# Attention: who normalises the probabilities, and which value products are rounded

## The chip, the cores and the metric

The kernel runs on one core of a Trainium2 chip. The time is what the device takes for one execution, in microseconds (us). Five engines work side by side, each with its own queue, in order: TensorE (PE) multiplies matrices and transposes, VectorE (DVE), ScalarE (ACT) and GpSimd (POOL) work element by element, and SyncE (SP) starts transfers. They wait for each other through semaphores. In this kernel GpSimd works on tiles in SBUF alone; VectorE and ScalarE also read the matmul results in PSUM.

## The reference, cut to what matters

The program is one decoder layer over 1024 tokens of width 1024: an RMS norm and an input projection, a retention part (8 heads), an attention part with three branches (8 query heads in 2 groups of key and value heads), an output projection, a gated MLP with a convolution, a gate from per-layer inputs, and a last norm. The change touches only the attention part:

```python
def masked_softmax(s, mask):
    s = jnp.where(mask, s.astype(jnp.float32), -jnp.inf)
    m = jnp.max(s, axis=-1, keepdims=True)
    m = jnp.where(jnp.isfinite(m), m, 0.0)
    e = jnp.exp(s - m)
    return e / jnp.maximum(jnp.sum(e, axis=-1, keepdims=True), 1e-30)
...
o = (gates[..., 0:1] * unblock(o_c) + gates[..., 1:2] * unblock(o_s)
     + gates[..., 2:3] * unblock(o_w))
```

Branch 0 attends to 63 compressed blocks, branch 1 to the selected blocks (with 16 blocks of 64 tokens and the 16 best chosen these are all tokens so far), branch 2 to a window of 512 tokens. Each has its own softmax, its own sum, and its own gate.

## The kernel before, in words

The work is in stages: projection with retention woven in, compression of keys and values, attention, output projection, MLP, final gate. The attention stage lies from about 447 to 771 us of the profiled execution.

It is tiled into 16 rounds `v`: token tile `t = v // 2` (128 queries) and key group `g = v % 2` (4 heads). Each round has 8 softmax steps `i`: head `r_ = i // 2`, and `i % 2` is 0 for branch 1 (up to 1024 columns) and 1 for branches 2 (up to 640 columns) and 0 (63 columns) together. All steps of all rounds have a running number `n = 8v + i`, and the whole stage is written as a list of slots, one for each `n`, by `plan_attention`. Every engine walks through the same slots in order.

For one step TensorE computes the scores into PSUM (`qk`, line 1206 and after), VectorE takes the row maxima and makes the bias from them (`row_max`, `exp_bias`), ScalarE writes `exp` into the SBUF tile `prob` and its row sum into `den` (`exponentials`; the accumulator read is a record of its own). One slot later VectorE guards the sum against zero (line 1673), takes the reciprocal (1678), and multiplies the probabilities in place by the reciprocal and the gate (1688, 1692 and 1695 for the three branches). `prob` has two places, for odd and for even rounds.

The value product comes one round later. Each tile of 128 keys (the last one of a round has the 63 compressed blocks) is a turn and an output. The turn (`p_turn`) is four transposes on TensorE, into one of three PSUM banks, recorded under line 1146. It waits on `norm_done` until all 8 steps of its round are normalised. Then the tile takes one of two ways:

- whole: ScalarE copies the bank to `ptw` in f32 (line 862), and TensorE multiplies in full f32, two records under line 1262
- not whole: ScalarE copies it rounded to `pth` (line 862), VectorE writes the remainder to `ptl` (`p_low`, recorded under line 1612), and TensorE makes two products of the rounded kind (lines 1264 and 1265)

Which way tile `j` of a round takes is said by one line:

```python
            return st[0] == "turn_p" and st[2] % 5 in (0, 2)
```

A round has 3, 5, 7, 9, 11, 12, 13, 14 tiles for token tiles 0 to 7. The turns and outputs of round `v` are spread over the slots `8v + 9` to `8v + 16`; in each slot TensorE first does these, then the scores of the step after. The scores of step `n` wait for the exponentials of step `n - 2`, whose PSUM banks they take.

GpSimd adds the squares at the start (line 609), issues the stores and loads of the projection and retention stages, and takes powers (-0.5) for the norms (lines 611, 643, 663, 667). In the attention stage it has nothing to do.

Of the kernel before, what the change touches and what calls it, by code (L numbers as in the profile page):

```python
# [7 lines left out]
ALU = mybir.AluOpType  # L8
ACT = mybir.ActivationFunctionType
AX_X = mybir.AxisListType.X  # L10
F32 = mybir.dt.float32
# [4 lines left out]
P = 128  # L16
S = 1024
D = 1024
NT = S // P
# [4 lines left out]
G = 2  # L24
RG = QH // G
CMP_BLOCK, CMP_STRIDE, CMP_HID = 32, 16, 256
NCMP = (S - CMP_BLOCK) // CMP_STRIDE + 1
CJ = CMP_BLOCK // 2
WIN_T = 4
# [5 lines left out]
SCALE = HD ** -0.5  # L35
# [13 lines left out]
C_DIAG = C_ID + P  # L49
# [5 lines left out]
C_CD = C_QD + RH  # L55
C_INV = C_CD + RH
C_HALF = C_INV + NA
C_N = C_HALF + NT


def constants():

    c = np.zeros((P, C_N), np.float32)
    p, f = np.arange(P)[:, None], np.arange(P)[None, :]
    c[:, C_ID:C_ID + P] = p == f
    c[:, C_DIAG:C_DIAG + P] = np.where(f <= p, 0.0, MASKED)
    c[:, C_FAR:C_FAR + P] = np.where(f > p, 0.0, MASKED)
    n = np.arange(NCMP)[None, None, :]
    t = np.arange(NT)[None, :, None] * P + np.arange(P)[:, None, None]
    cm = np.zeros((P, NT, HD))  # L70
    cm[:, :, :NCMP] = np.where(n * CMP_STRIDE + CMP_BLOCK - 1 <= t, 0.0, MASKED)
    c[:, C_CMP:C_CMP + NT * HD] = cm.reshape(P, -1)
    log_g = np.log1p(-np.exp2(-5.0 - np.arange(RH)))
    for h in range(RH):
        c[:, C_DT + h * P:C_DT + (h + 1) * P] = np.where(f >= p, np.exp(np.maximum(f - p, 0) * log_g[h]), 0.0)
        c[:, C_KD + h] = np.exp((P - 1.0 - np.arange(P)) * log_g[h])
        c[:, C_QD + h] = np.exp((np.arange(P) + 1.0) * log_g[h])
        c[:, C_CD + h] = np.exp(P * log_g[h])
    for at, half, theta in ((0, ROPE_R, 10000.0), (ROPE_R, ROPE_N, 500000.0)):
        e = -np.arange(half, dtype=np.float32) / np.float32(half)  # L80
        c[:, C_INV + at:C_INV + at + half] = np.power(np.float32(theta), e)
    c[:, C_HALF:] = -0.5
    return c


# [23 lines left out]
def build(nc, xt, x, pt, pos, cst_d, wmix_d, wffn_d, gnw, w_in, cpos, ck_w1, ck_w2, cv_w1, cv_w2,  # L109
# [8 lines left out]
    with ctx:  # L118
        def sem(name):
            return ctx.enter_context(nc.semaphore(name))  # L120
# [102 lines left out]
        comb = a.put("comb", [P, 2, 2 * P], F32)  # L223
        mx = a.put("mx", [P, 4, 2], F32)
        nb = a.put("nb", [P, 4, 2], F32)
        den = a.put("den", [P, 4, 2], F32)
        rd = a.put("rd", [P, 4, 2], F32)
        rd2 = a.put("rd2", [P, 4, 2], F32)
        assert a.at <= 229344, a.at


# [63 lines left out]
        cst_in = sem("cst_in")  # L295
        xt_in, w_in_s = sems("xt_in", XR), sems("w_in", RR)

        cst_r, cst_m = sem("cst_r"), sem("cst_m")
        xh_done, sq_done, xl_done = sem("xh_done"), sem("sq_done"), sem("xl_done")
        acc_done, ss_done, ms_done, rstd_done = sem("acc_done"), sem("ss_done"), sem("ms_done"), sem("rstd_done")  # L300
        red_done, sin_done = sem("red_done"), sem("sin_done")
# [50 lines left out]
        def ret_slots(s, k, table):  # L352
# [17 lines left out]
        tr_full, tr_h, tr_l = sem("tr_full"), sem("tr_h"), sem("tr_l")  # L370
        qk_done, nb_done, exp_done, norm_done, pv_done = (
            sem("qk_done"), sem("nb_done"), sem("exp_done"), sem("norm_done"), sem("pv_done"))
        swap_done, csum_done, nsah_done, nsal_done = sem("swap_done"), sem("csum_done"), sem("nsah_done"), sem("nsal_done")

        h_in, wfb_in = sem("h_in"), sem("wfb_in")
# [55 lines left out]
        def whole(st):  # L431

            return st[0] == "turn_p" and st[2] % 5 in (0, 2)

        outs_of = {(v, j): n for n, (v, j) in enumerate(st[1:] for st in plan if st[0] == "output")}

# [165 lines left out]
        def _(pool):  # L604
# [48 lines left out]
            for s in range(NS + 1):  # L653
                for k in range(NK):
# [3 lines left out]
                        ret_load(0)  # L658
                    ret_slots(s, k, table)

            for t in range(NT):
                pool.wait_ge(hms_done, t + 1)
                nc.gpsimd.tensor_tensor(hst[:, 2, t:t + 1], hst[:, 1, t:t + 1], cst[:, C_HALF:C_HALF + 1], ALU.pow) \
                    .then_inc(hrs_done, 1)
# [6 lines left out]
        def _(act):  # L671
# [164 lines left out]
            def exponentials(v, i):  # L836
                n, t = 2 * RG * v + i, v // G
                r_, br = divmod(i, 2)
                act.wait_ge(nb_done, n + 1)
                if v >= 2:  # L840
                    act.wait_ge(tr_full, turns_of["turn_p", v - 2, len(key_tiles(v - 2)) - 1] + 1)
                s_, pr = ps[:, 2 * br:2 * br + 2, :].rearrange("p a n -> p (a n)"), prob[:, v % 2, r_]
                m = n % 4
                if br == 0:
                    nc.scalar.activation(pr[:, 0:(t + 1) * P], s_[:, 0:(t + 1) * P], ACT.Exp, bias=nb[:, m, 0:1],
                                         scale=SCALE, accum_out=den[:, m, 0:1]).then_inc(exp_done, 1)
                else:
                    w = (t - max(0, t - WIN_T) + 1) * P
                    nc.scalar.activation(pr[:, S:S + w], s_[:, 0:w], ACT.Exp, bias=nb[:, m, 0:1], scale=SCALE,
                                         accum_out=den[:, m, 0:1])  # L850
                    at = S + (WIN_T + 1) * P
                    nc.scalar.activation(pr[:, at:at + NCMP], s_[:, 5 * P:5 * P + NCMP], ACT.Exp, bias=nb[:, m, 1:2],  # L852
                                         scale=SCALE, accum_out=den[:, m, 1:2]).then_inc(exp_done, 1)

            def p_high(st):
                at = place_of[st]
# [150 lines left out]
        def _(pe):  # L1007
# [32 lines left out]

            def sum_squares():
                pe.wait_ge(acc_done, NK - 1)
                pe.wait_ge(cst_m, 1)
                for t in range(NT):
                    mm = nc.tensor.matmul(ps[:, 4, t:t + 1], xacc[:, t * P:(t + 1) * P], ones[:], start=True, stop=True)
                mm.then_inc(ss_done, 1)
# [188 lines left out]
            def p_turn(st):  # L1235
                v, j = st[1:]
                _, _, at, w = key_tiles(v)[j]
                pe.wait_ge(norm_done, 2 * RG * (v + 1))
                turn_free(st)
                for r_ in range(RG):  # L1240
                    mm = transpose_f(ps[0:w, turn_bank(st), r_ * P:(r_ + 1) * P], prob[:, v % 2, r_, at:at + w])
                mm.then_inc(tr_full, 1)
# [158 lines left out]
        def _(dve):  # L1401
# [8 lines left out]
            def mark(ins):  # L1410

                count[0] += 1
                ins.then_inc(dve_chain, 1)
                return count[0]

            dve.wait_ge(cst_in, 48)
            chain(nc.vector.memset(ones[:], 1.0))
            nc.vector.tensor_copy(ident_b[:], ident_f).then_inc(cst_m, 1)
            nc.vector.tensor_copy(masks_b[:], cst[:, C_DIAG:C_DT]).then_inc(cst_m, 1)

            def split_w(j):
                dve.wait_ge(wh_done, j + 1)
# [244 lines left out]
                dve.wait_ge(dve_chain, maxima)  # L1667
                nc.vector.tensor_scalar(nb[:, m, 0:w], mx[:, m, 0:w], FLOOR, -SCALE, ALU.max, ALU.mult).then_inc(nb_done, 1)

            def guard_sum(v, i):  # L1670
                n, w = 2 * RG * v + i, 1 + i % 2
                dve.wait_ge(exp_done, n + 1)
                return mark(nc.vector.tensor_scalar(rd[:, n % 4, 0:w], den[:, n % 4, 0:w], 1e-30, None, ALU.max))

            def invert_sum(v, i, guarded):
                m, w = (2 * RG * v + i) % 4, 1 + i % 2
                dve.wait_ge(dve_chain, guarded)
                return mark(nc.vector.reciprocal(rd2[:, m, 0:w], rd[:, m, 0:w]))

            def normalize(v, i, inverted):  # L1680

                n, (t, g_), (r_, br) = 2 * RG * v + i, divmod(v, G), divmod(i, 2)
                m, hd = n % 4, g_ * RG + r_
                dve.wait_ge(dve_chain, inverted)
                pr = prob[:, v % 2, r_]
                if br == 0:
                    p_ = pr[:, 0:(t + 1) * P]
                    nc.vector.tensor_scalar(p_, p_, rd2[:, m, 0:1], gates[:, t, hd, 1:2], ALU.mult, ALU.mult).then_inc(norm_done, 1)
                else:
                    width = (t - max(0, t - WIN_T) + 1) * P  # L1690
                    p_ = pr[:, S:S + width]
                    nc.vector.tensor_scalar(p_, p_, rd2[:, m, 0:1], gates[:, t, hd, 2:3], ALU.mult, ALU.mult)
                    at = S + (WIN_T + 1) * P
                    p_ = pr[:, at:at + NCMP]
                    nc.vector.tensor_scalar(p_, p_, rd2[:, m, 1:2], gates[:, t, hd, 0:1], ALU.mult, ALU.mult).then_inc(norm_done, 1)

            def p_low(st):
                at = place_of[st]
                w = key_tiles(st[1])[st[2]][3]
# [28 lines left out]
            for n, slot in enumerate(slots):  # L1728
                lows = [st for st in slot if st[0] in ("turn_p", "turn_ret") and not whole(st)]
                if n < 2 * RG * NV:  # L1730
                    maxima = row_max(*divmod(n, 2 * RG))
                if 0 < n <= 2 * RG * NV:
                    guarded = guard_sum(*divmod(n - 1, 2 * RG))
                if n < 2 * RG * NV:
                    exp_bias(*divmod(n, 2 * RG), maxima)
                if 0 < n <= 2 * RG * NV:
                    inverted = invert_sum(*divmod(n - 1, 2 * RG), guarded)
                for st in lows:
                    {"turn_p": p_low, "turn_ret": ret_low}[st[0]](st)
                if 0 < n <= 2 * RG * NV:  # L1740
                    normalize(*divmod(n - 1, 2 * RG), inverted)
                for st in slot:
                    {"split_q": q_split_low, "sum": add_parts, "combine": nsa_low}.get(st[0], skip)(st)

# [175 lines left out]
```

## Time and profile before

| | |
|---|---|
| median of 3 runs | 1783.72 us (1783.25 to 1783.78) |
| span of the profiled execution | 1782.5 us, first to last instruction |
| its own time | not given beside the span; the runs' times are 0.75 to 1.28 us above it |
| TensorE busy | 1653.7 us (93%) |
| VectorE busy | 1054.2 us (59%) |
| ScalarE busy | 628.0 us (35%) |
| GpSimd busy | 109.5 us (6%) |
| attention stage | about 447 to 771 us |

How to read it: the busy time of TensorE comes from modelled ends of pipelined matmuls, and short overlaps are in it. The shares are means over stages with different limits, so the stage's own windows count more than they do. "E <- R" in a view is an engine that sat idle until R was done.

### The profile page before, as it was taken

How to read it: one execution, taken by the hardware profiler on the slowest of the kernel's cores; microseconds unless marked ns; L12 is line 12 of the kernel's file. 1: busy time of each engine (PE TensorE's matmuls, PEld its weight loads, DVE VectorE, ACT ScalarE, POOL GpSimd, SP SyncE). 2: the span in 40 equal slices, each digit the busy share in tenths (PEclk: the TensorE clock that was granted, in tenths of full speed). 3: DMA queues.
4: the chain of work that ended last, by engine and by line, in shares of the span. 5: the costliest groups of instructions: out<-in, count | busy, mean ns of one | idle time of the engine just before them, and what ended most of it. 6: DMA issues, size and time to landing. Idle time of an engine off the chain costs nothing.

```text
span 1782.5 us, 22209 instructions
## 1 busy us (share of the span) xinstructions
PE 1653.7 (93%) x8157; PEld 1334.8 (75%) x8157; DVE 1054.2 (59%) x2073; ACT 628.0 (35%) x1161; POOL 109.5 (6%) x132
## 2 busy tenths in 40 slices
PE   3999999998789999989899999999999999996894
PEld 1888888888656776668788888888888888885673
DVE  7542556565799999842545556556555555556233
ACT  5103443344577777731422212212212212213121
POOL 4101112121000000000100000000000000000002
PEclk9999999999699999999899999999999999998997
DMA  5233323225000000130211211211111112102002
GB/s 188 90 100 120 102 93 110 78 80 200 24 22 16 13 13 1 65 138 0 75 55 36 71 35 38 68 35 46 60 35 52 54 35 57 61 1 95 0 36 82
DMA packets 47850, 110.57 MB, mean 62 GB/s; under 512 B 8864, under 2 KB 17056, under 8 KB 47776
## 3 DMA queue, kind: packets, MB, share of 16 engines
q1 hardware_dynamic: 40352, 85.47, 14.8%
q0 software_dynamic: 7424, 24.12, 4.0%
q8 instruction: 45, 0.74, 0.2%
q14 instruction: 29, 0.24, 0.0%
HBM read 89.65 MB, written 19.92 MB: 61 GB/s over the span
## 4 chain that ended last, share of the span: by engine, by line
PE 81%; DVE 11%; ACT 3%; DMA 2%; issue 2%; POOL 0%; POOLq 0%; SPq 0%; DVEq 0%; ACTq 0%
PE ps L1325 27%; PE ps L1011 13%; PE ps L1012 13%; PE ps L1013 13%; PE ps L1146 3%; PE ps L1262 3%; PE ps L1219 2%; PE ps L1225 1%; PE ps L1264 1%; PE ps L1016 1%; DVE xtl L1444 1%; PE ps L1169 1%; DVE wl L1424 1%; DVE htl L1612 1%; PE ps L1265 1%
## 5 line engine op out<-in xcount | busy, mean ns | idle before, releaser
L1798 DVE TENSOR_TENSOR h<-h,ps 128x512 f32<-128x512 f32 x352 | 236.1, 685 | 156.1 <-PE ps L1013 154.8
L1325 PE MATMUL ps<-hth,wuh 128*128 128x512 f32 x704 | 218.6, 392 | 3.1 <-DVE wul L1612 3.1
L1325 PE MATMUL ps<-htl,wuh 128*128 128x512 f32 x704 | 219.0, 392 | 0.0
L1325 PE MATMUL ps<-hth,wul 128*128 128x512 f32 x704 | 218.6, 392 | 0.0
L1011 PE MATMUL ps<-wh,xth 128*128 128x512 f32 (+1 forms) x448 | 187.5, 419 | 31.1 <-DVE wl L1424 29.7
L1013 PE MATMUL ps<-wh,xtl 128*128 128x512 f32 (+1 forms) x448 | 171.2, 382 | 0.0
L1012 PE MATMUL ps<-wl,xth 128*128 128x512 f32 (+1 forms) x448 | 170.7, 381 | 0.0
L952 ACT ACTIVATE ffh<-ffa 128x1024 fp32r<-128x1024 f32 x22 | 23.3, 1059 | 385.1 <-DVE ffa L1815 385.1
L1325 PEld LDWEIGHTS ps<-hth,wuh 128*128 128x128 f32 x704 | 132.4, 188 | 32.9 <-issue 3.3
L1325 PEld LDWEIGHTS ps<-hth,wul 128*128 128x128 f32 x704 | 132.7, 188 | 29.4
L1325 PEld LDWEIGHTS ps<-htl,wuh 128*128 128x128 f32 x704 | 132.5, 188 | 28.8
L1011 PE MATMUL ps<-wdh,ffh 128*128 128x512 f32 x352 | 139.5, 396 | 4.3 <-DVE ffl L1612 4.3
L1012 PE MATMUL ps<-wdl,ffh 128*128 128x512 f32 x352 | 140.3, 399 | 0.0
L1013 PE MATMUL ps<-wdh,ffl 128*128 128x512 f32 x352 | 139.5, 396 | 0.0
L1011 PEld LDWEIGHTS ps<-wh,xth 128*128 128x128 f32 x448 | 85.8, 192 | 44.4 <-issue 26.8
L1805 DVE SCALAR_TENSOR_TENSOR act__149<-gate,taps,act__149 128x1024 f32<-128x1024 f32 x22 | 28.3, 1285 | 129.2 <-ACT act__149 L945 129.2
L1146 PE MATMUL ps<-cst,prob 128*128 128x128 f32 (+1 forms) x592 | 89.3, 279 | 9.7 <-DVE retl L1612 7.8
L1013 PEld LDWEIGHTS ps<-wh,xtl 128*128 128x128 f32 x448 | 85.5, 191 | 16.2
L1219 PE MATMUL ps<-aks,aqt 128*128 128x512 f32 (+3 forms) x192 | 82.3, 429 | 15.4 <-ACT prob L852 13.5
L1146 PEld LDWEIGHTS ps<-cst,prob 128*128 128x128 f32 (+1 forms) x592 | 69.8, 143 | 34.0 <-issue 24.5
L1012 PEld LDWEIGHTS ps<-wl,xth 128*128 128x128 f32 x448 | 86.3, 193 | 8.2
L1011 PEld LDWEIGHTS ps<-wdh,ffh 128*128 128x128 f32 x352 | 66.5, 189 | 20.6 <-DVE ffl L1612 4.7
(263 smaller groups left out, 3174.8 us busy)
## 6 DMA issues: line engine op xcount, KB each, us to landing
wuraw<-in_w_up SPq DMA_DIRECT2D x44, 512.0 KB, 5.4
wraw<-in_w_in SPq DMA_DIRECT2D x48, 256.0 KB, 3.2
proj_d<-stage POOLq DMA_DIRECT2D x48, 256.0 KB, 2.3
wdraw<-in_w_down SPq DMA_DIRECT2D x22, 512.0 KB, 3.5
rin<-proj_d POOLq DMA_DIRECT2D x32, 256.0 KB, 4.0
xraw<-in_xt SPq DMA_DIRECT2D x8, 512.0 KB, 4.9
h<-in_x SPq DMA_DIRECT2D x1, 4096.0 KB, 12.8
owraw<-in_w_out SPq DMA_DIRECT2D x16, 256.0 KB, 3.1
```

Of the source, the lines that this page charges most:

```text
L952: nc.scalar.activation(ffh[:, u], ffa[:], ACT.Copy).then_inc(ffh_done, 1)
L1011: first = nc.tensor.matmul(out, wh_, xh_, start=start, stop=False)
L1012: nc.tensor.matmul(out, wh_, xl_, start=False, stop=False)
L1013: return first, nc.tensor.matmul(out, wl_, xh_, start=False, stop=stop)
L1016: return nc.tensor.transpose(out.bitcast(F32R), in_, ident_r[:])
L1146: return nc.tensor.transpose(out, in_, ident_f[0:n, 0:n])
L1169: mm = nc.tensor.matmul(ps[:, 6 + i, half * G * NCMP:(half + 1) * G * NCMP], cw1[:, i, j, half * P:(half + 1) * P], cb[:, i, j], start=(j ...
L1219: nc.tensor.matmul(ps[:, bank, 0:w], q_, aks[:, br, g_, at:at + w], start=True, stop=False)
L1262: mm = nc.tensor.matmul(out_, vals.bitcast(F32), ptw[0:w, at], start=first, stop=last)
L1325: mm = nc.tensor.matmul(ps[:, 2 * part + half, :], w_, x_[:, k, half * 512:(half + 1) * 512], start=(k == 0 and i == 0), stop=(k == NK - 1 ...
L1798: nc.vector.tensor_tensor(hh, hh, ps[:, 4 + o_ % 4, :], ALU.add).then_inc(dn_add, 1)
L1805: nc.vector.scalar_tensor_tensor(act_[:], gate[:, 1:S + 1], taps[:, u, 1:2], act_[:], ALU.mult, ALU.add).then_inc(conv_mid, 1)
```

## The change

The guard, the reciprocal and the scaling leave VectorE and go to GpSimd, once for each head instead of once for each step. The three sums of a head now lie side by side in `den` (4 places of 3), and `rd`, `rd2` have the same form. GpSimd waits for the head's second step, guards the three sums, raises them to the power -1 with a constant of three -1 columns, and scales the three branches of `prob` in place. `norm_done` now counts heads. ScalarE waits for the guard of the head four before, whose place in `den` it takes. Two semaphores of the start of the program are used again, and one is dropped. And one tile in five, not two, is whole.

```diff
@@ constants: three columns of -1.0 are added
+C_NEG = C_HALF + NT
+C_N = C_NEG + 3
...
+        guard_done, inv_done, G0 = red_done, sin_done, 2
...
-            return st[0] == "turn_p" and st[2] % 5 in (0, 2)
+            return st[0] == "turn_p" and st[2] % 5 == 0
...
+            def invert_sums(v, r_):
+                n = RG * v + r_
+                pool.wait_ge(exp_done, 2 * n + 2)
+                nc.gpsimd.tensor_scalar(rd[:, n % 4], den[:, n % 4], 1e-30, None, ALU.max).then_inc(guard_done, 1)
+                pool.wait_ge(guard_done, G0 + n + 1)
+                nc.gpsimd.tensor_tensor(rd2[:, n % 4], rd[:, n % 4], cst[:, C_NEG:C_NEG + 3], ALU.pow).then_inc(inv_done, 1)
+
+            def normalize(v, r_):
+                n, (t, g_) = RG * v + r_, divmod(v, G)
+                hd = g_ * RG + r_
+                pool.wait_ge(inv_done, G0 + n + 1)
+                pr, wt, gt = prob[:, v % 2, r_], rd2[:, n % 4], gates[:, t, hd]
+                p_ = pr[:, 0:(t + 1) * P]
+                nc.gpsimd.tensor_scalar(p_, p_, wt[:, 1:2], gt[:, 1:2], ALU.mult, ALU.mult)
+                p_ = pr[:, S:S + (t - max(0, t - WIN_T) + 1) * P]
+                nc.gpsimd.tensor_scalar(p_, p_, wt[:, 2:3], gt[:, 2:3], ALU.mult, ALU.mult)
+                at = S + (WIN_T + 1) * P
+                p_ = pr[:, at:at + NCMP]
+                nc.gpsimd.tensor_scalar(p_, p_, wt[:, 0:1], gt[:, 0:1], ALU.mult, ALU.mult).then_inc(norm_done, 1)
+
+            for v in range(NV):
+                for r_ in range(RG):
+                    invert_sums(v, r_)
+                    normalize(v, r_)
...
@@ exponentials, on ScalarE
+                if n >= 8:
+                    act.wait_ge(guard_done, G0 + n // 2 - 3)
...
-                                         scale=SCALE, accum_out=den[:, m, 0:1]).then_inc(exp_done, 1)
+                                         scale=SCALE, accum_out=den[:, m2, 1:2]).then_inc(exp_done, 1)
...
@@ sum_squares and p_turn, on TensorE
-                pe.wait_ge(cst_m, 1)
+                pe.wait_ge(dve_chain, 1)
...
-                pe.wait_ge(norm_done, 2 * RG * (v + 1))
+                pe.wait_ge(norm_done, RG * (v + 1))
...
@@ the slots of VectorE; guard_sum, invert_sum and normalize are deleted there
                     maxima = row_max(*divmod(n, 2 * RG))
-                if 0 < n <= 2 * RG * NV:
-                    guarded = guard_sum(*divmod(n - 1, 2 * RG))
-                if n < 2 * RG * NV:
                     exp_bias(*divmod(n, 2 * RG), maxima)
-                if 0 < n <= 2 * RG * NV:
-                    inverted = invert_sum(*divmod(n - 1, 2 * RG), guarded)
                 for st in lows:
                     {"turn_p": p_low, "turn_ret": ret_low}[st[0]](st)
-                if 0 < n <= 2 * RG * NV:
-                    normalize(*divmod(n - 1, 2 * RG), inverted)
```

## Rows read from the trace of the kernel before

**Rows 1.** Chain that ended last, shares of the span by engine.

```profile
PE 81%; DVE 11%; ACT 3%; DMA 2%; issue 2%; POOL 0%; POOLq 0%; SPq 0%; DVEq 0%; ACTq 0%
```

**Rows 2.** Windows: length; PE, PEld, DVE, ACT, POOL busy; granted clock; DMA; GB/s.

```profile
464.40:522.20 57.80, 48.18 (x263) 34.67 (x263) 49.78 (x210) 38.55 (x132) 0.00 (x0) 0.85 0.06 19
522.20:592.10 69.90, 64.94 (x387) 44.77 (x386) 68.52 (x230) 54.28 (x151) 0.00 (x0) 1.00 0.06 16
592.10:634.50 42.40, 41.43 (x259) 30.49 (x258) 40.60 (x118) 32.46 (x82) 0.00 (x0) 1.00 0.05 14
634.50:680.00 45.50, 43.98 (x271) 32.00 (x269) 42.55 (x119) 34.75 (x84) 0.00 (x0) 1.00 0.04 13
680.00:729.90 49.90, 47.53 (x282) 33.65 (x281) 45.14 (x121) 36.41 (x85) 0.00 (x0) 1.00 0.00 1
729.90:754.40 24.50, 22.12 (x128) 15.38 (x126) 21.71 (x58) 17.86 (x42) 0.00 (x0) 1.00 0.17 62
```

**Rows 3.** Chain of waits, 680 to 700 us: start, length on the chain, what.

```profile
684.40 0.91 PE ps L1262 x2
...
685.98 0.23 PE ps L1265
```

**Rows 4.** Timeline: last sum and first turn of rounds 0, 4, 9, 14, 15.

```profile
461.67 0.20 ACT L852 ACTIVATION_READ_ACCUMULATOR prob<-ps,nb 128x1 f32 x1
...
464.42 0.85 PE L1146 MATMUL ps<-cst,prob 128*128 128x128 f32 x3
...
520.67 0.20 ACT L852 ACTIVATION_READ_ACCUMULATOR prob<-ps,nb 128x1 f32 x1
...
522.22 0.49 PE L1146 MATMUL ps<-cst,prob 128*128 128x128 f32 x3
...
611.31 0.20 ACT L852 ACTIVATION_READ_ACCUMULATOR prob<-ps,nb 128x1 f32 x1
...
613.50 0.31 PE L1146 MATMUL ps<-cst,prob 128*128 128x128 f32 x1
...
726.42 0.20 ACT L852 ACTIVATION_READ_ACCUMULATOR prob<-ps,nb 128x1 f32 x1
...
729.93 0.27 PE L1146 MATMUL ps<-cst,prob 128*128 128x128 f32 x1
...
752.65 0.20 ACT L852 ACTIVATION_READ_ACCUMULATOR prob<-ps,nb 128x1 f32 x1
...
753.14 0.15 DVE L1673 TENSOR_SCALAR rd<-den 128x2 f32<-128x2 f32 x1
...
754.06 0.31 DVE L1695 TENSOR_SCALAR prob<-prob,rd,gates 128x63 f32<-128x63 f32 x1
...
754.43 0.44 PE L1146 MATMUL ps<-cst,prob 128*128 128x128 f32 x2 [1.15 <-DVE prob L1695]
```

**Rows 5.** Groups of VectorE, 447 to 771 us: busy, mean ns, idle before.

```profile
L1612 DVE TENSOR_TENSOR ptl<-ps,pth 128x512 fp32r<-128x512 f32 (+1 forms) x82 | 55.7, 682 | 19.5 <-ACT pth L862 18.4
...
L1688 DVE TENSOR_SCALAR prob<-prob,rd,gates 128x128 f32<-128x128 f32 (+7 forms) x64 | 36.7, 573 | 0.9
L1692 DVE TENSOR_SCALAR prob<-prob,rd,gates 128x640 f32<-128x640 f32 (+4 forms) x64 | 33.6, 525 | 1.2
...
L1678 DVE RECIPROCAL rd<-rd 128x1 f32<-128x1 f32 (+1 forms) x128 | 20.6, 161 | 0.0
L1695 DVE TENSOR_SCALAR prob<-prob,rd,gates 128x63 f32<-128x63 f32 x64 | 19.7, 307 | 0.0
L1673 DVE TENSOR_SCALAR rd<-den 128x1 f32<-128x1 f32 (+1 forms) x128 | 19.3, 151 | 0.8 <-ACT prob L852 0.5
```

**Rows 6.** Single lines of GpSimd: count, ns min/median/max, start us, forms.

```profile
L663 POOL TENSOR_TENSOR hst<-hst,cst x8: 539/1515/1525, 834.9 to 868.9; 128x1 f32<-128x1 f32 x8
...
L643 POOL TENSOR_TENSOR gst<-gst,cst x8: 1663/1666/2048, 195.9 to 412.7; 128x8 f32<-128x8 f32 x8
...
L609 POOL TENSOR_TENSOR xacc<-xacc,xsq x6: 2593/2713/3154, 16.1 to 35.6; 128x1024 f32<-128x1024 f32 x6
```

More of the change, by code:

```diff
@@ L57 @@
 C_HALF = C_INV + NA
-C_N = C_HALF + NT
+C_NEG = C_HALF + NT
+C_N = C_NEG + 3
 def constants():
@@ L81, in constants @@
         c[:, C_INV + at:C_INV + at + half] = np.power(np.float32(theta), e)
-    c[:, C_HALF:] = -0.5
+    c[:, C_HALF:C_NEG] = -0.5
+    c[:, C_NEG:] = -1.0
     return c
@@ L225, in build @@
         nb = a.put("nb", [P, 4, 2], F32)
-        den = a.put("den", [P, 4, 2], F32)
-        rd = a.put("rd", [P, 4, 2], F32)
-        rd2 = a.put("rd2", [P, 4, 2], F32)
+        den = a.put("den", [P, 4, 3], F32)
+        rd = a.put("rd", [P, 4, 3], F32)
+        rd2 = a.put("rd2", [P, 4, 3], F32)
         assert a.at <= 229344, a.at
@@ L296, in build @@
         xt_in, w_in_s = sems("xt_in", XR), sems("w_in", RR)
-        cst_r, cst_m = sem("cst_r"), sem("cst_m")
+        cst_r = sem("cst_r")
         xh_done, sq_done, xl_done = sem("xh_done"), sem("sq_done"), sem("xl_done")
@@ L842, in exponentials @@
                 s_, pr = ps[:, 2 * br:2 * br + 2, :].rearrange("p a n -> p (a n)"), prob[:, v % 2, r_]
-                m = n % 4
+                m, m2 = n % 4, n // 2 % 4
                 if br == 0:
                     nc.scalar.activation(pr[:, 0:(t + 1) * P], s_[:, 0:(t + 1) * P], ACT.Exp, bias=nb[:, m, 0:1],
-                                         scale=SCALE, accum_out=den[:, m, 0:1]).then_inc(exp_done, 1)
+                                         scale=SCALE, accum_out=den[:, m2, 1:2]).then_inc(exp_done, 1)
                 else:
@@ L849, in exponentials @@
                     nc.scalar.activation(pr[:, S:S + w], s_[:, 0:w], ACT.Exp, bias=nb[:, m, 0:1], scale=SCALE,
-                                         accum_out=den[:, m, 0:1])
+                                         accum_out=den[:, m2, 2:3])
                     at = S + (WIN_T + 1) * P
                     nc.scalar.activation(pr[:, at:at + NCMP], s_[:, 5 * P:5 * P + NCMP], ACT.Exp, bias=nb[:, m, 1:2],
-                                         scale=SCALE, accum_out=den[:, m, 1:2]).then_inc(exp_done, 1)
+                                         scale=SCALE, accum_out=den[:, m2, 0:1]).then_inc(exp_done, 1)
             def p_high(st):
@@ L1417, in _ @@
             chain(nc.vector.memset(ones[:], 1.0))
-            nc.vector.tensor_copy(ident_b[:], ident_f).then_inc(cst_m, 1)
-            nc.vector.tensor_copy(masks_b[:], cst[:, C_DIAG:C_DT]).then_inc(cst_m, 1)
+            nc.vector.tensor_copy(ident_b[:], ident_f)
+            nc.vector.tensor_copy(masks_b[:], cst[:, C_DIAG:C_DT])
             def split_w(j):
@@ L1668, in exp_bias @@
                 nc.vector.tensor_scalar(nb[:, m, 0:w], mx[:, m, 0:w], FLOOR, -SCALE, ALU.max, ALU.mult).then_inc(nb_done, 1)
[L1670 to L1695, printed above, removed]
             def p_low(st):
```

## The prediction

> **What bounds the kernel now.** I read the chain of waits first. Over the whole span it is 81% TensorE and 0% GpSimd [rows 1], so only a change of TensorE's own time, or of what it waits for, moves the end. The change touches the attention stage alone, so the next view is the table of windows over that stage, cut where the first probability turn of rounds 0, 4, 8, 10, 12, 14 and 15 starts [rows 2]. A round is one token tile and one key group. The reader should see three things. Up to 592 us VectorE is busy 118.3 of 127.7 us and TensorE 113.1, so TensorE has room there. After 592 us TensorE is busy 155.1 of 162.3 us, all but full, and VectorE 150.0. GpSimd does nothing at all. The rounds take 14.4, 17.5, 21.2, 22.8, 25.0 and 24.5 us (window over rounds in it: 4, 4, 2, 2, 2, 1).
>
> Then I read how the softmax hands over to the value product. TensorE may not turn any probability of a round before all eight softmaxes of the round are normalised. The gap from the last sum of a round (the accumulator read of line 852) to the first turn is 2.55 us in round 0, 1.35 in round 4, 1.99 in round 9, 3.3 in round 14, 1.58 in round 15 [rows 4]. Between those I interpolate: 1.35 for rounds 1 to 4, 1.7 for 5 to 8, 2.2 for 9 and 10, 2.6 for 11 and 12, 3.1 for 13 and 14. TensorE spends this gap on the next scores and the last outputs of the round before, so what matters below is how much longer than that the new gap is.
>
> **Part 1: VectorE is relieved.** Removed are 128 guards, 128 reciprocals and 192 normalisations: 19.3 + 20.6 + 36.7 + 33.6 + 19.7 = 129.9 us [rows 5]. Added are the remainders of the tiles that are no longer whole: of j mod 5 in (0, 2), the tiles with j mod 5 = 2 change, 1, 1, 1, 2, 2, 2, 3, 3 per round for token tiles 0 to 7, times two groups = 30. At 682 ns [rows 5] that is 20.5 us. VectorE ends 109 us lighter in a stage of some 320 us. What this can return is at most TensorE's idle time per round [rows 2]: 14.4 - 12.0 = 2.4, 17.5 - 16.2 = 1.2, 0.5, 0.8, 1.2 and 2.4 us. Some of it is the head of the dependency from scores to maximum to exponential, which stays. I take half: 1.2, 0.6, 0.25, 0.4, 0.6, 1.2.
>
> **Part 2: fewer whole products.** On the chain a whole value product (two passes, line 1262) holds TensorE 0.91 us; a rounded one (lines 1264 and 1265) is two matmuls of 0.23, 0.46 [rows 3]. Each of the 30 saves 0.45, 13.5 us in all; per round of the windows 0.45, 0.7, 0.9, 0.9, 1.35, 1.35. The turn, and the copy on ScalarE, stay. The 20.5 us on VectorE are covered by the 129.9 that leave it; if VectorE were still full they would cost what they save.
>
> **Part 3: GpSimd does the work.** Per head and round, 64 times: a guard of 3 columns, a power of 3 columns that waits for it, and three scalings in place that wait for the power. Columns: (t+1)x128, up to 640, and 63, so 319, 575, 831, 1087, 1343, 1471, 1599, 1727 for token tiles 0 to 7, 71,616 in all. The trace has no GpSimd instruction of the scaling's form, so its price must be bounded.
> - Power: 1.515 us median for one column, 1.666 for eight; the shortest is 0.539 [rows 6]. I take 1.55, the median of one column and a little more.
> - Guard: from below VectorE's 0.151 [rows 5], from above the power's 1.515. I take 0.54, the shortest small instruction on this engine.
> - Scaling: from below VectorE's own 90.0 us over all columns, 1.26 ns a column with its fixed part [rows 5]. From above the add of 1024 columns, 2.71 us median or 2.65 ns a column [rows 6], with 0.54 of fixed time on top. The add reads two tensors and the scaling one, so I take half the add's slope, 1.35 ns, and 0.3 us fixed for each of the three (between 0 and 0.54): an estimate.
> - Handing over: in round 15 the guard starts 0.29 us after the last sum, and the turn 0.06 after the last scaling ends [rows 4]; with the hop from guard to reciprocal and the next, each like that 0.06, this makes 0.47; I keep 0.45.
>
> The new gap from the last sum to the first turn is L = 0.45 + 0.54 + 1.55 + 0.9 + 1.35 ns x columns = 3.44 us + 1.35 ns x columns: 3.9 us at tile 0, 5.8 at tile 7. The wait stands in TensorE's queue in front of all turns and outputs of the round and all later scores. During it ScalarE and VectorE can only finish the softmaxes whose scores are already out. After that they starve, so the excess over the old gap is lost nearly in full. GpSimd's own occupancy, 3.1 us + 1.35 ns x columns a head, is 15.5 us a round at tile 1 and 21.7 at tile 7. It keeps up, barely in the early rounds, so the head before does not delay the last one by much.
>
> Per round, new gap less old, less part 2, less part 1:
> - round 0: 3.9 - 2.55 = +1.3
> - rounds 1 to 4: 4.2 - 1.35 - 0.45 - 1.2 = +1.2, four times +4.8
> - rounds 5 to 8: 4.9 - 1.7 - 0.7 - 0.6 = +1.9, four times +7.6
> - rounds 9, 10: 5.35 - 2.2 - 0.9 - 0.25 = +2.0, twice +4.0
> - rounds 11, 12: 5.5 - 2.6 - 0.9 - 0.4 = +1.6, twice +3.2
> - rounds 13, 14: 5.7 - 3.1 - 1.35 - 0.6 = +0.65, twice +1.3
> - round 15: 5.8 - 1.6 - 1.35 - 1.2 = +1.65; its own outputs, behind the gap, -1.35
>
> Sum +22.5 us. The profiled execution's span is 1782.5 us; the runs' median, 1783.7, lies 1.2 us above it, which I leave as it is. Forecast: 1782.5 + 22.5 + 1.2 = 1806 us.
>
> The rest costs nothing: TensorE's wait for the ones moves to another semaphore of the same event, and GpSimd has no work of its own in the stage that the new loop could delay.
>
> Two rules of the Trainium skill pull the scaling's price apart. GPSIMD Engine Reference, section 4.1 Engine selection with section 1, says that one-input elementwise work on this engine runs at about one column a cycle of 1.2 GHz, 0.83 ns; by that the gap shrinks by 0.3 to 0.9 us a round and the estimate would be 1797. The same page's section 8 Key points says that VectorE is about twice as fast at elementwise work; twice VectorE's 90 us are 26 us more than my scaling, 0.4 us a head, and the estimate would be 1813. No row of this trace decides between them.
>
> **Rivals.** *A, the relief wins.* GpSimd is about as fast as the lower bounds: guard 0.15, shortest power 0.54, VectorE's own scaling times (1.4 us a head on average). The gap is then 2.2 to 2.9 us, and the stage gets nearly all of TensorE's idle time back. Per round -1.6 (x4), -0.95 (x4), -0.75 (x2), -1.25 (x2), -2.2 (x2), -2.0, the first -0.3 and the tail -1.35: -22 us, 1762. For it: VectorE is all but full before 592 us while TensorE is not. Against it: the median of the eight one-column powers is 2.8 times the shortest [rows 6].
> *B, GpSimd becomes the bound.* It decides once a head costs it more than a quarter of a round, 3.6 us early and 6.2 late. With 0.54 of fixed time on each scaling and 2.0 ns a column a head costs 3.9 us + 2.0 ns x columns; a round takes 20.0, 24.1, 26.7, 27.7, 28.7, 29.3 us against the 14.4 to 24.5 of now, +85 us with the ends: 1869. With the add's full 2.65 ns it is near 1920. For it: my own price already fills it in the early rounds. Against it: the three scalings wait for nothing between them, so fixed parts may overlap.
> *C, no change.* Gap and relief cancel at L about 1.4 us lower than mine on average: 1784.
> That the change does not do what it says I exclude: every step of it is in the diff.
>
> **How the numbers follow.** Forecast (1790 to 1840) 0.42, A 0.28, C 0.07, B and what lies above 1840 0.23. A measurement here can tell about 0.2%, 3.6 us, from no change. So faster 0.28, same 0.07, slower 0.65. The range leaves out the low end of A and the upper part of B: 1762 to 1868. The forecast's own range is 1790 to 1840.
>
> **What would show it.** In the new profile GpSimd should be busy some 230 to 310 us in the stage; the guard should show near 0.54, the power near 1.55, the scaling of 640 columns near 1.2 us. VectorE should fall to 55 to 65% of the stage. TensorE's largest wait should be line 1146's turns on the scaling of 63 columns, 2 to 3.5 us in each of the 16 rounds. Line 1262 should have 72 records and not 132. I am wrong if the power or the small scalings cost half or twice this: every 1 us on a head's chain moves the end by about 16 us, and more once GpSimd is full.

## The result and the profile after

The changed kernel takes 1822.6 us (1818.6 to 1828.0, 4 runs) against 1783.75 us: 1.0214 times the time before, interval 1.019 to 1.0237. The forecast was 1806, slower, and the range held it. The direction and the gap as its mechanism were right, but of the terms of the sum one was nearly twice too large and another had the wrong sign.

The chain of waits of the changed kernel by engine, answering [rows 1]: GpSimd is on it now.

```profile
PE 81%; DVE 8%; ACT 4%; POOL 3%; issue 3%; DMA 2%; POOLq 0%; ACTq 0%; SPq 0%; DVEq 0%
```

The windows of the changed kernel, cut at the first turns of rounds 0, 4, 8, 10, 12, 14 and 15 as in [rows 2], with the same columns:

```profile
464.65:533.80 69.15, 55.70 (x262) 42.57 (x261) 36.36 (x106) 39.10 (x134) 42.26 (x81) 0.70 0.05 14
533.80:618.60 84.80, 68.73 (x387) 50.07 (x385) 55.93 (x125) 55.04 (x151) 49.02 (x81) 0.92 0.05 13
618.60:666.80 48.20, 42.38 (x256) 31.89 (x256) 32.19 (x66) 32.31 (x81) 26.77 (x41) 0.96 0.04 12
666.80:714.00 47.20, 42.99 (x268) 31.92 (x268) 33.81 (x67) 33.75 (x82) 27.41 (x41) 1.00 0.04 12
714.00:764.60 50.60, 45.94 (x280) 33.54 (x280) 36.47 (x69) 35.97 (x86) 28.24 (x41) 1.00 0.01 1
764.60:791.40 26.80, 21.26 (x126) 15.30 (x126) 17.32 (x33) 17.37 (x41) 14.23 (x21) 0.96 0.26 97
```

The six windows were 57.8, 69.9, 42.4, 45.5, 49.9 and 24.5 us long. They are 11.4, 14.9, 5.8, 1.7, 0.7 and 2.3 longer now, 36.8 together, so most of the loss lies in the rounds up to 618 us; the two ends of the stage make the rest of 39. VectorE fell from 268 busy us to 212 in them. TensorE does not get the room: it is busy 277 of 327 us where it was 268 of 290. The granted clock in the first window fell from 0.85 to 0.70.

The trace now has the price of GpSimd's work, which [rows 6] could only bound. Groups of the changed kernel (busy us, mean ns of one | idle before):

```profile
L670 POOL TENSOR_TENSOR rd<-rd,cst 128x3 f32<-128x3 f32 x64 | 56.5, 883 | 5.3
L684 POOL TENSOR_SCALAR prob<-prob,rd,gates 128x63 f32<-128x63 f32 x64 | 27.2, 425 | 0.0
L668 POOL TENSOR_SCALAR rd<-den 128x3 f32<-128x3 f32 x64 | 14.5, 227 | 163.8 <-ACT prob L884 163.7
L679 POOL TENSOR_SCALAR prob<-prob,rd,gates 128x1024 f32<-128x1024 f32 x8 | 9.6, 1205 | 0.8
L679 POOL TENSOR_SCALAR prob<-prob,rd,gates 128x128 f32<-128x128 f32 x8 | 3.6, 453 | 0.8
```

The guard takes 0.23 us and the power 0.88. The scaling is (1205 - 453) / 896 = 0.84 ns a column and 0.35 fixed. What a head costs shows in the last hand-over of the stage, round 15 of the changed kernel, beside [rows 4]. Timeline (start, us, engine, line):

```profile
787.57 0.20 ACT L884 ACTIVATION_READ_ACCUMULATOR prob<-ps,nb 128x1 f32 x1
787.85 0.23 POOL L668 TENSOR_SCALAR rd<-den 128x3 f32<-128x3 f32 x1 [2.44 <-ACT prob L884]
788.16 0.88 POOL L670 TENSOR_TENSOR rd<-rd,cst 128x3 f32<-128x3 f32 x1
789.15 1.20 POOL L679 TENSOR_SCALAR prob<-prob,rd,gates 128x1024 f32<-128x1024 f32 x1
790.33 0.88 POOL L681 TENSOR_SCALAR prob<-prob,rd,gates 128x640 f32<-128x640 f32 x1
791.18 0.41 POOL L684 TENSOR_SCALAR prob<-prob,rd,gates 128x63 f32<-128x63 f32 x1
...
791.64 0.69 PE L1178 MATMUL ps<-cst,prob 128*128 128x128 f32 x2 [3.44 <-POOL prob L684]
```

From the last sum (787.77) to the first turn it is 3.87 us, where it was 1.58. Read the same way in all 16 rounds, the gap goes from 2.9 us in round 0 to 3.9 in the last ones. Its sum is 56.6 us, against 32.4 before.

A second loss shows in ScalarE's waits (engine, tile and line, waited for: us, times, longest). In the kernel before, its copies of turned tiles waited for the turn alone:

```profile
ACT pth L862 <- PE ps L1146: 21.5, 42, 1.1
ACT ptw L862 <- PE ps L1146: 17.9, 30, 1.1
```

In the changed kernel:

```profile
ACT pth L894 <- PE ps L1297: 55.6, 43, 3.7
ACT ptw L894 <- PE ps L1178: 20.8, 17, 2.5
ACT prob L881 <- DVE nb L1700: 18.3, 20, 1.8
ACT pth L894 <- PE ps L1178: 14.1, 33, 1.5
```

The first row is new. Line 1297 is the second half of a rounded value product. The copy waits for it because a rounded tile needs a free place in `pth` and `ptl`, and there are two. Timeline of the changed kernel:

```profile
718.16 0.60 PE L1178 MATMUL ps<-cst,prob 128*128 128x128 f32 x4
...
718.83 0.40 PE L1297 MATMUL ps<-ptl,av 128*128 128x512 f32 x1
719.32 0.60 ACT L894 ACTIVATE pth<-ps 128x512 fp32r<-128x512 f32 x1 [1.11 <-PE ps L1297]
719.81 1.00 ACT L877 ACTIVATE prob<-ps,nb 128x896 f32<-128x896 f32 x1
```

The turn of 718.16 is done by 718.8, but the copy starts only after the product of an older tile, and an exponential stands behind the copy. Two places for rounded tiles were enough while at most two rounded tiles followed each other (tiles 1; 3 and 4; 6; 8 and 9). With one in five whole, tiles 1 to 4 follow each other. Tile 3 needs the place of tile 1, whose product TensorE issues only after the turn of tile 3. ScalarE's new wait for GpSimd's guard of the head four before does not show in its waits.

### The profile page after: what moved, and what is told of

It is laid out like the page before. It is cut to its first block, busy times and chain, and to the rows that moved or that the text cites. A ratio compares the mean times of both kernels' runs of the same rounds, so it can differ in the third digit from the quotient of the medians.

```text
span 1822.0 us, 22119 instructions
## 1 busy us (share of the span) xinstructions
PE 1664.8 (91%) x8157; PEld 1351.1 (74%) x8157; DVE 994.7 (55%) x1655; ACT 626.8 (34%) x1161; POOL 306.9 (17%) x452
## 4 chain that ended last, share of the span: by engine, by line
PE 81%; DVE 8%; ACT 4%; POOL 3%; issue 3%; DMA 2%; POOLq 0%; ACTq 0%; SPq 0%; DVEq 0%
PE ps L1357 27%; PE ps L1043 13%; PE ps L1045 13%; PE ps L1044 13%; PE ps L1178 4%; PE ps L1251 2%; PE ps L1294 2%; PE ps L1257 2%; PE ps L1296 1%; PE ps L1297 1%; DVE htl L1644 1%; DVE xtl L1476 1%; PE ps L1201 1%; PE ps L1048 1%; DVE wl L1456 1%
## 5 line engine op out<-in xcount | busy, mean ns | idle before, releaser
L697 POOL TENSOR_TENSOR fst<-fst,cst 128x1 f32<-128x1 f32 x8 | 11.2, 1399 | 893.4 <-DVE fst L1846 893.4
L1178 PE MATMUL ps<-cst,prob 128*128 128x128 f32 (+1 forms) x592 | 99.2, 302 | 25.2 <-POOL prob L684 24.6
L1644 DVE TENSOR_TENSOR ptl<-ps,pth 128x512 fp32r<-128x512 f32 (+1 forms) x112 | 76.7, 689 | 79.3 <-ACT pth L894 78.8
L1178 PEld LDWEIGHTS ps<-cst,prob 128*128 128x128 f32 (+1 forms) x592 | 77.8, 156 | 45.4 <-POOL prob L684 27.8
```

What stands on the lines that cost most here:

```text
L1178: return nc.tensor.transpose(out, in_, ident_f[0:n, 0:n])
L1644: return nc.vector.tensor_tensor(out_, full, high.bitcast(F32), ALU.subtract)
```

## The experiments

The times of a group of four were taken with runs of the kernel before on the same chip: 1782.2 us for E1 to E4, 1782.9 for the rest.

**E1, GpSimd's part alone.**

```diff
-            return st[0] == "turn_p" and st[2] % 5 == 0
+            return st[0] == "turn_p" and st[2] % 5 in (0, 2)
```

> The changed kernel with two tiles in five whole again, so GpSimd's part of the change alone. Theory (the loss is the longer gap before each round's first turn, and the half clock that follows the gaps; fewer whole products give part of it back): TensorE gets 13.5 us of work back, of which some falls into idle time: 1828 to 1836 us, gaps unchanged at 2.9 to 3.9 us. Rival (the rounded products are the loss, since each needs a remainder from VectorE behind ScalarE's copy): at or below 1815 us.

Measured 1804.2 us, 1.0125 (1.0102 to 1.0147). The rival's number was met: whole products back in place take 18 us off. E5, E6 and E8 show that its reason, the remainder from VectorE, was not the one. The gaps stay (sum 56.2 us), and ScalarE's copies to `pth` wait no more for line 1297. Taken apart in this order, 22 us are GpSimd's part and 18 the rounded tiles.

**E2, the rounded tiles alone.** The same line changed the other way, in the kernel before.

> The kernel before with one tile in five whole, so the second part of the change alone, with VectorE still normalising. Theory (VectorE, full up to 592 us and at 92% after, pays for the 30 remainders about what TensorE saves): 1778 to 1788 us. If TensorE's saving counted in full: 1770 us. Rival (the rounded products are the loss): 1795 us or more.

Measured 1813.6 us, 1.0177 (1.016 to 1.0194): 31 us of loss with VectorE normalising as before. ScalarE's wait is here as well, in the waits of E2:

```profile
ACT pth L862 <- PE ps L1265: 48.7, 41, 2.6
ACT prob L849 <- DVE nb L1668: 28.1, 31, 1.7
...
PE ps L1219 <- ACT prob L852: 19.2, 25, 1.7
PE ps L1219 <- ACT prob L845: 12.5, 13, 1.8
```

TensorE's own wait for exponentials (line 1219) was 10.6 and 0.3 us in the kernel before, and is 31.7 here. The theory as I had put it, no loss from rounding, had fallen, and these rows gave the new one: the places.

Alone the two parts cost 22 us (E1) and 31 (E2), together 39. So they overlap by some 14 us, and in the other order the rounded tiles are 31 and GpSimd's part 9 (1822.6 against 1813.6).

**E3, work in the gap.** The changed kernel with seven more matmuls for TensorE ahead of the wait at the start of a round.

```diff
-                pe.wait_ge(norm_done, RG * (v + 1))
                 turn_free(st)
+                if j == 0 and v < NV - 1:
+                    for _ in range(7):
+                        nc.tensor.matmul(ps[:, turn_bank(st), :], av2[:, 0, 0, 0], aks[:, 0, 0, 0:512], start=True, stop=True)
+                pe.wait_ge(norm_done, RG * (v + 1))
```

> The changed kernel with seven rounded matmuls of 128x512 more in TensorE's queue, into the bank that the first turn of rounds 0 to 14 will take, ahead of its wait on the normalisation: some 1.6 us of work a round inside the gap; their results are overwritten. The gap itself stays. Clock theory (about 20 of the 39 us are TensorE at half clock after the gaps): the granted clock in the stage rises to that of before and the time falls to 1800 to 1808 us. Rival (the clock only follows the idle time and costs little, the gap is all): 1820 us or more, since the added work can only delay.

Measured 1816.9 us, 1.0205 (1.0182 to 1.0227), 5.7 less than the changed kernel. Neither number was met, and the 5.7 us are hardly clear of noise: the runs lie between 1814.1 and 1819.9 us, those of the changed kernel between 1818.6 and 1828.0. The windows over the whole stage, first the kernel before, then the changed kernel, then E3:

```profile
453.00:771.00 318.00, 292.39 (x1705) 209.67 (x1704) 283.66 (x910) 228.61 (x613) 0.00 (x0) 0.95 0.07 25
```

```profile
453.00:809.00 356.00, 301.82 (x1703) 225.26 (x1702) 224.54 (x494) 226.95 (x611) 197.68 (x320) 0.89 0.07 22
```

```profile
453.00:800.00 347.00, 307.77 (x1811) 226.68 (x1810) 223.57 (x494) 225.85 (x613) 197.87 (x320) 0.96 0.07 23
```

The granted clock is back at 0.96, where it was 0.95 before, but the time falls by far less than the clock theory said. The added matmuls also lengthen the gaps by 7.2 us in sum (63.8 against 56.6). If each us of them costs the 1.1 us of E10, the clock is worth up to some 13 us of the 39: an estimate, with the noise of the 5.7 in it. It is not the 20 that I had expected.

**E4, the last head on VectorE.** GpSimd guards, inverts and scales heads 0 to 2 of each round, VectorE head 3 in the slot after its second step, with a semaphore of its own.

```diff
-                for r_ in range(RG):
+                for r_ in range(RG - 1):
                     invert_sums(v, r_)
...
-                pe.wait_ge(norm_done, RG * (v + 1))
+                pe.wait_ge(norm_done, (RG - 1) * (v + 1))
+                pe.wait_ge(last_norm, v + 1)
```

> The changed kernel with the fourth head of each round guarded, inverted and scaled on VectorE as before, GpSimd keeping the first three. Gap theory (what counts is only the time from a round's last sum to its first turn): the gap falls from 2.9 to 3.9 back to 1.2 to 2.2 us, VectorE stays 75 us lighter than before, and the time falls to 1765 to 1785 us. Rival (GpSimd's three heads still slow VectorE or ScalarE down beside them, or the remainders are the loss): 1800 us or more.

Measured 1800.8 us, 1.0103 (1.0087 to 1.012), which is the rival's number and not the theory's. The gaps fell to 1.4 to 2.9 us (sum 35.4) and the time by 22, as much as GpSimd's part had cost. The theory lacked the other loss, the rounded tiles: ScalarE's copies still wait 53.3 us for their products.

**E5, three places.** The changed kernel with

```diff
-        NPT = 2
+        NPT = 3
...
-        NPW = 2
+        NPW = 1
```

> The changed kernel with three places for rounded tiles and one for whole ones, instead of two and two. New theory (with one tile in five whole, four rounded ones follow each other; two places make ScalarE's copy of a tile wait for the product of the tile two before, 55.6 us in the trace, and the exponentials stand behind it in ScalarE's queue): this wait falls below 10 us and the time to 1785 to 1800 us, at or under the 1804 of the same kernel with two tiles in five whole. Rival (each rounded tile costs more by itself, in VectorE's remainder and ScalarE's and VectorE's hand-over): 1815 us or more.

Measured 1796.7 us, 1.007 (1.0049 to 1.009): 26 us less than with two places. The wait of ScalarE's copies to `pth` for line 1297 is gone:

```profile
ACT pth L894 <- PE ps L1178: 41.2, 80, 1.8
ACT ptw L894 <- PE ps L1178: 25.2, 33, 2.4
```

It is also 7.5 us under E1, which differs from it by the 30 tiles and the places: the rounded products do save here, more than half of what I had counted.

**E6, three places in the kernel before.** The edit of E2 and the edit of E5.

> The kernel before with one tile in five whole and three places for rounded tiles, one for whole. Places theory: the 31 us that one in five cost with two places go, 1776 to 1786 us; VectorE, full, decides whether anything is gained. Rival (the rounded tile itself): 1800 us or more.

Measured 1785.6 us, 1.0016 (1.0007 to 1.0026). 28 of the 31 us of E2 go, and nothing is gained: VectorE is busy 297.9 us of the 317 between 453 and 770. That is what part 2 of the prediction said of a full VectorE: the remainders then cost what the products save.

**E7, GpSimd's part without its gap.** The edits of E1 and E4.

> Two tiles in five whole, GpSimd for the first three heads, VectorE for the last: the part of the change on the normalisation with its gap taken away. Gap theory (the 22 us of GpSimd's part alone are the longer gap): the gap is 1.2 to 2.8 us again, and the time is 1770 to 1782 us, at or below the kernel before. Rival (something else in GpSimd's work, such as a hold on VectorE's SBUF access, costs it): 1792 us or more.

Measured 1782.7 us, 0.9998 (0.9985 to 1.0011), 0.7 us above the range that was expected. The gaps are 1.5 to 3.3 us (sum 36.0), and the 22 us of E1 are gone. VectorE's relief by three heads in four shortens the first rounds (rounds 1 to 3 by 2.4, 2.3 and 0.9 us) and no late one, and does not show in the time.

**E8, never three rounded tiles in a row.** The kernel before, with

```diff
-            return st[0] == "turn_p" and st[2] % 5 in (0, 2)
+            return st[0] == "turn_p" and st[2] % 3 == 0
```

> The kernel before with every third tile whole (54 whole tiles instead of 66, 12 more rounded), so that never more than two rounded tiles follow each other, with two places as before. Places theory: no tile waits for a place, 1777 to 1785 us. Rival (about 1 us for each tile made rounded, as 31 us for 30 tiles would say): 1793 us or more.

Measured 1783.3 us, 0.9994 (0.9982 to 1.0006): 12 more rounded tiles and no change. With E6 this shows that it is not the number of rounded tiles that costs, but how many follow each other for the places there are.

**E9, nothing to normalise.** The guard, the reciprocal and the scaling are left out of the kernel before, and the turns wait for the exponentials, so the probabilities stay unnormalised.

> The kernel before with the guard, the reciprocal and the scaling left out, so the probabilities stay unnormalised; the turns wait on the exponentials instead. It shows what VectorE's relief of 130 us can bring at most, with no gap in exchange. If TensorE's idle time comes back as the prediction took it, half of it and more: 1755 to 1770 us. If scores, maxima and exponentials keep TensorE waiting anyway: 1774 us or more.

Measured 1773.2 us, 0.995 (0.9933 to 0.9967), between the two numbers and nearer to the second. This is all that VectorE's relief can bring with tiles as before: 10 us. Windows of E9 over the stage:

```profile
453.00:758.00 305.00, 285.72 (x1705) 205.91 (x1704) 198.09 (x465) 226.26 (x612) 0.00 (x0) 0.97 0.08 26
```

VectorE is down to 65%, and TensorE is busy 285.7 of 305 us: it was the bound, or close to it, nearly all the time.

**E10, the power twice.** E1 with

```diff
                 nc.gpsimd.tensor_tensor(rd2[:, n % 4], rd[:, n % 4], cst[:, C_NEG:C_NEG + 3], ALU.pow).then_inc(inv_done, 1)
+                pool.wait_ge(inv_done, G0 + 2 * n + 1)
+                nc.gpsimd.tensor_tensor(rd2[:, n % 4], rd[:, n % 4], cst[:, C_NEG:C_NEG + 3], ALU.pow).then_inc(inv_done, 1)
...
-                pool.wait_ge(inv_done, G0 + n + 1)
+                pool.wait_ge(inv_done, G0 + 2 * n + 2)
```

> Two tiles in five whole, GpSimd for all heads, and its power done twice, the second after the first: the gap before each round's first turn is 0.9 to 1.0 us longer than in the same kernel with one power (1804 us). Gap theory: one us on the gap is 16 us on the end, 1817 to 1822 us. Rival (part of the longer gap is hidden by work that is late anyway): 1806 to 1812 us.

Measured 1834.2 us, 1.0288 (1.0271 to 1.0305), 30 us over E1 and outside both expectations. TensorE's wait for the scaling, first E1, then E10:

```profile
PE ps L1178 <- POOL prob L684: 23.0, 16, 3.4
```

```profile
PE ps L1180 <- POOL prob L686: 49.0, 16, 5.8
```

The wait grew by 26.0 us and the sum of the gaps by 26.3, from a second power of 0.85 us: in late rounds a gap is 0.95 us longer, in early ones up to 3.8. There the last head waits for GpSimd to finish the heads before it, as in round 1 of E10:

```profile
476.76 0.20 ACT L886 ACTIVATION_READ_ACCUMULATOR prob<-ps,nb 128x1 f32 x1
...
479.37 0.41 POOL L686 TENSOR_SCALAR prob<-prob,rd,gates 128x63 f32<-128x63 f32 x1
...
479.86 0.48 POOL L668 TENSOR_SCALAR rd<-den 128x3 f32<-128x3 f32 x1
...
483.67 1.12 PE L1180 MATMUL ps<-cst,prob 128*128 128x128 f32 x4 [5.78 <-POOL prob L686]
```

The sum is there at 476.96, and its guard starts 2.9 us later, once the head before is scaled. In total 1 us of gap is 1.1 us of time (30 for 26.3), and a us on every head's chain is more than 1 us of gap: these 0.85 us on it cost 30, where the prediction's rule of 16 us for each said 14.

**E11, both losses away.** One in five whole, three places (E5) and the last head on VectorE (E4).

> One tile in five whole with three places for rounded tiles, GpSimd for the first three heads and VectorE for the last: both losses taken away. If the two are independent: 1796.7 less the 21.5 us that the last head's move brought at two in five, 1775 us. If the rounded products gain nothing once TensorE waits for ScalarE: 1780 to 1785 us.

Measured 1776.1 us, 0.9959 (0.9946 to 0.9971). It beats both kernels, by 0.4% and by 2.5%. Against E6, the same tiles and places with all heads on VectorE, it is 9.5 us less, although its gaps are 6.2 us longer in sum (35.4 against 29.2). So with more rounded tiles VectorE's relief is worth something.

**E12, the turns a slot later.** E1 with

```diff
-                base = per * (v + 1) + 1
+                base = per * (v + 1) + 2
```

> Two tiles in five whole, GpSimd for all heads, and the turns and outputs of every round one slot later in the plan, so that TensorE does one more softmax step's scores inside the gap. Gap theory: most of the 22 us come back, since the gap is filled and no longer waited for: 1782 to 1792 us. Rival (the gap must be short, since what is behind it is late by it): 1800 us or more.

Measured 1777.3 us, 0.9971 (0.9961 to 0.9981), below what was expected. GpSimd keeps all four heads. TensorE's wait for the scaling in E12:

```profile
PE ps L1178 <- POOL prob L684: 6.3, 7, 1.7
```

It was 23.0 us in E1. The time from the last sum to the first turn is even longer (68.0 us in sum against 56.2), but the scores of one more step lie in it. One number in the plan is worth 27 us here. How much of it is the gap stays open: the result is 5.6 us under the kernel before, and no run has the kernel before with its turns a slot later.

## Why the prediction was right, and where its steps were not

**The gap was the mechanism.** The first turns of the rounds (line 1178) wait for the scaling of 63 columns in 15 of 16 rounds:

```profile
PE ps L1178 <- POOL prob L684: 24.6, 15, 3.4
```

E4 and E7 take the gap away and the time goes with it, E10 lengthens it and the time follows. That the excess is "lost nearly in full" holds too: E10 gives 1.1 us for each. The size of the gap was overrated: by my list the gaps would sum to 79 us, and they sum to 56.6. The increase is 24 us, not 47.

**The prices of part 3** are the reason. The guard was 0.23 us where I took 0.54 from the shortest power. The power was 0.88 where I took the median of one column, 1.55; three columns cost less here than the median of one column in [rows 6], so that median was no lower bound for the operation. For the scaling I halved the slope of the add, 1.35 ns, and it is 0.84. The Trainium skill (GPSIMD Engine Reference, section 4.1 Engine selection) says of work with one input only that it runs at roughly line rate. With the clock of its section 1 Specifications, 1.2 GHz, one column a cycle would be 0.83 ns, an estimate: the trace agrees with it. (By this rule the gap shrinks by 0.2 us at 319 columns; the 0.3 that I gave as the least is that of 575.) The other rule I cited from the Trainium skill (GPSIMD Engine Reference, section 8 Key points, VectorE about twice as fast) does not hold for this form: 129.3 us on GpSimd for what took 90.0 on VectorE, 1.4 times.

**Part 1, the relief of VectorE**, was counted at 10.9 us. E9, with all of the work gone, gives 9.7; E7, with three quarters moved, gives nothing beside a gap sum that is 3.6 us longer. At E10's 1.1 us for each us of gap, the relief comes to some 4 us in E7 and in E1 alike (23.8 us of gap make 26, measured 22): an estimate. So with tiles as before the 10.9 were too many. With one tile in five whole and three places it is more: E11 is 9.5 us under E6 at longer gaps.

**Part 2 failed.** I wrote that each of the 30 rounded products saves 0.45 us, 13.5 in all, and that the remainders are covered. That the products save can be seen with three places: -7.5 us (E5 against E1). That the remainders need a VectorE with room holds too, since E6 gains nothing and E11 does. The two places of `pth` and `ptl` I had not looked at: the step changes not only how many tiles are rounded but how many follow each other. I took it that the tile always has a place to go to. The effect of rounding the 30 tiles is +18 us beside GpSimd's part (E1) and +31 without it (E2), where I had -13.5.

**So the sum**: predicted +36 for GpSimd's part (47 less 10.9) and -13.5 for the rounded tiles, +22.5; measured +22 and +18, +39. GpSimd's part came out 14 us too high and the tiles 31 too low. That the measured time still lies in the range is luck: the two errors have opposite signs.

**The clock** was not a term of mine. The granted clock has two levels, 0.50 (1.2 GHz) and 1.00 (2.4 GHz), and the mean over the stage is 0.89 against 0.95. E3 puts its share at up to some 13 us, part of the two terms above and not on top. The same twelve transposes at the start of a round, on the chain of the changed kernel, at 642 and at 690 us, each with the window around it:

```profile
642.36 2.82 PE ps L1178 x12
```

```profile
642.30:645.20 2.90, 2.84 (x13) 2.84 (x14) 0.34 (x2) 1.19 (x2) 0.01 (x1) 0.50 0.15 43
```

```profile
690.43 1.53 PE ps L1178 x12
```

```profile
690.40:692.00 1.60, 1.56 (x13) 1.56 (x14) 0.86 (x3) 0.87 (x2) 0.00 (x0) 1.00 0.27 82
```

Both follow a wait for GpSimd. In the 4.3 us before the first TensorE was busy 2.4 us, in the 4.4 us before the second 3.1.

**Rivals.** A (1762) took a gap of 2.2 to 2.9 us; the measured 2.9 to 3.9 lies between that and my 3.9 to 5.8. It was wrong all the same, since it also counted the relief in full, which is at most 10 us with tiles as before, and the rounded tiles as a gain. B, GpSimd as the bound, did not come: it is busy 197.7 of 356 us. Rival B's point of decision can be seen in the early rounds of E10, where a head's chain waits for the one before.

What stays open is how the loss of the rounded tiles divides between the exponentials that come late and the half clock behind them. No run here has the places without their effect on the clock.

## What to carry to other kernels

Before work moves to an idle engine, find the last piece of it that someone waits for, and price the hand-over, not the occupancy: here the whole stage waited for one head in each of 16 rounds. Leave that piece on the fast engine, or put other work that is due anyway into the wait. When a choice between two ways of handling tiles is changed, look at the longest run of each way and at its buffer places, not only at the counts.

## What the runs showed of the hardware

A short VectorE instruction can be held until a GpSimd one ends. The maximum's bias took 161 ns in the mean before and 206 in the changed kernel. The group before, the group in the changed kernel, and a timeline of the latter:

```profile
L1668 DVE TENSOR_SCALAR nb<-mx 128x1 f32<-128x1 f32 (+1 forms) x128 | 20.6, 161 | 0.0
```

```profile
L1700 DVE TENSOR_SCALAR nb<-mx 128x1 f32<-128x1 f32 (+1 forms) x128 | 26.3, 206 | 4.4
```

```profile
784.15 0.88 POOL L681 TENSOR_SCALAR prob<-prob,rd,gates 128x640 f32<-128x640 f32 x1
...
784.44 0.62 DVE L1700 TENSOR_SCALAR nb<-mx 128x2 f32<-128x2 f32 x1
```

It takes 0.62 us and not 0.17, and ends at 785.06, 0.03 us after GpSimd's scaling, which ends at 785.03. Of the 64 biases of two columns in the changed kernel 18 took more than 0.25 us, up to 0.76, and each of the 18 ends 0.02 to 0.03 us after a scaling of GpSimd that began before it. Of the 64 with one column none took more than 0.16. VectorE's reductions, which read PSUM, show nothing of it (752 ns in the mean against 751). The Trainium skill (SBUF — State Buffer, section Who interferes with whom) says that VectorE's forms with two ports, which `tensor_scalar` can take, are blocked wholly while GpSimd holds the shared pair, and reductions never; the rows agree. All of it is 5.7 us of VectorE's time. Three of the held ones lie on the chain that ended last, 0.46, 0.57 and 0.50 us long; the others do not show on it.
